# Hybrid four-mixer layer: v and z of mixer C as a seven-product unit, rope matmuls issued one by one, B's levels merged by predicated copies, output projection as seven products

## The chip, the cores and the metric

The kernel runs on 1 core of one Trainium2 chip. Its time is the device time of one execution in microseconds, the median of the runs shown. All data is float32, and every logical matmul is issued to the array as two instructions, so the profile counts two matmuls for one in the code.

## What is computed

Two layers (`DEPTH = 2`) on a sequence of 1024 rows of width 1024. Each layer does, cut to what matters here:

```python
h = _rmsnorm(x, norm_g[l])
p = h @ w_in[l]                       # all input projections and the merge gates
oa = _chunk_band_attention(...) * silu(az)
ob = _hgrn2(...) * silu(bz)           # mixer B, a decayed linear recurrence in chunks of 64
oc = _dsa(_rope(cq), _rope(ck), cv, _rope(cqi), _rope(cki), cwi) * silu(cz)   # indexer, top 256 keys, attention
od = _rwkv7(...) * silu(dz)
y = sum over branches of sigmoid(g) * (o @ w_branch[l, b])
x = x + y @ w_out[l]                  # output projection, 1024 x 1024 by 1024 x 1024
```

and after both layers a last RMSNorm.

## The kernel before

The normalised input stands transposed in `hT` (128 partitions, 8 blocks of the model width, 1024 rows), the weights pass through the ring `wr` of four slots of 256 columns. The engines' programs are written by hand, one list for each engine and layer, in the order C, D, B, A of the mixers, and then the tail. They meet at semaphores. `Jobs` keeps PSUM banks: `open` waits until the bank was emptied, `filled` signals the reader, `emptied` gives it back. Banks G[0] and G[1] (512 columns each) take the products of projections in turn, T and O and the pair S2 the mixers' small work.

**Fills.** Projections that no mixer waits for at once are cut into fill units of one 512-column matmul (or two 256-column ones), and `pe_fill(pe, n)` issues the next n of them wherever TensorE (PE) would else wait for another engine. Numbers in the constants (`TOPK_FILL`, `QK_FILL`, `D_FILL`, `B_FILL`) say how many at each place; `FILL_ORDER` says in which order projections come, and the merge gates take the rest. What is left after mixer A is issued in one run in `pe_tail`. Most fills are done by a scheme of seven products for a 2 by 2 block product (`PRODUCTS`), in place of eight: four matmuls to a product, with block sums of the weights (`t1` to `t4`) and of `hT` (`s1` to `s4`) made by GpSimd (POOL) in `pool_w_sums` and `pool_h_sums`. ScalarE (ACT) drains the products in `act_fills`, up to the mark at which it stands in its own program, and POOL adds half of them to their places. "Rows" units are two blocks of 256 columns (v and z of a mixer) as 256-column matmuls with four pairs of row tiles.

**Mixer C.** PE projects the index key, the index queries (blocks `("C", 0)`, `("C", 1)`, in `pe_proj_t`), then v and z (blocks 2 and 3, `pe_proj_n`, 64 matmuls of 512 columns). `pe_rope` makes the rotated half of a tile by one matmul into the single bank T, which VectorE (DVE) or, for q and k, ACT and POOL, must empty before the next. Then come the index scores: `for n, (i, hp, c, w) in enumerate(index_units)`, with 2 fills at each second unit. DVE sums them over heads, then searches the 256th largest score of each row bit by bit from 31 to 0 (six counts over up to 1024 columns and three small instructions for a bit), while PE issues fills; then PE starts the attention (`scores`, `turn`, `values`), whose first softmax on DVE needs the search done.

**Mixer B.** For each half m: decayed keys and queries for six levels (DVE differences, ACT exponentials, `L1499`), state sums (`adds`), a scan of 15 linked steps over chunks, then for each of 8 row tiles seven small product blocks, one for a level and one for the diagonal. DVE multiplies all seven by 0/1 masks (`near7`) and adds them up (L1591 and L1598); PE multiplies the result with v.

**Tail.** 64 branch products (two matmuls each) go through four banks; DVE multiplies each with its gate and adds it into `yT`, the half of the rows first. Then the output projection: for each of 8 row tiles two column halves by eight matmuls of 512 columns, DVE adds the old x (L914), and ACT and DVE make the next norm in `act_norm` and `dve_norm`.

## Time and profile before

| | |
|---|---|
| median of 3 runs | 3275.61 us (3271.96 to 3279.4) |
| profiled execution | 3285.09 us, its span 3283.1 us |
| PE busy | 3003.6 us, 91% of the span |
| DVE, ACT, POOL busy | 1661.7, 823.4, 658.9 us |
| mean granted TensorE clock | 0.968 |
| PE waits for ACT's drain of a probability tile (L971) | 51.1 us in 71 waits |
| PE waits for B's merged tile (L1463) | 21.1 us in 24 waits |
| PE waits before rope matmuls (L1217) | 31.1 us |

Busy time is a union over overlapping instructions, so a group's busy time divided by its count is the pitch at which it streamed; the mean duration beside it contains the latency of the array. PE is the engine with the least idle time, but it is not idle evenly: it stands at places where one of its small results goes through DVE or ACT and back.

### The profile page before, as it was taken

The page shows a single profiled execution, that of the slowest core. Times are in us where ns is not written, and L with a number is a line of the kernel's source. Part 1 is how long each engine was busy: PE and PEld are TensorE (multiplying, and loading weights), DVE is VectorE, ACT ScalarE, POOL GpSimd, SP SyncE. Part 2 cuts the span into 40 slices and gives each one's busy share as a digit, 9 for nine tenths or more (in the row PEclk, how much of TensorE's full clock was granted, in tenths as well). Part 3 has the DMA queues.
Part 4 walks back from the last instruction along what each step waited for, and adds up shares of the span by engine and source line. Part 5 has one row for each costly group of instructions (what it writes and reads, how often), then busy time and mean ns, then how long its engine had stood idle before and what let it go on. Part 6 is the DMA issues. An engine that isn't in the chain of part 4 may idle for free. (4 is left out here: it accounts for less than half of the span.)

```text
span 3283.1 us, 46212 instructions
## 1 busy us (share of the span) xinstructions
PE 3003.6 (91%) x18760; PEld 1547.7 (47%) x18760; DVE 1661.7 (51%) x3186; ACT 823.4 (25%) x1554; POOL 658.9 (20%) x476
## 2 busy tenths in 40 slices
PE   6999997999998889899989999879999887898997
PEld 3444444457543446444443444444665444554443
DVE  2169974753347741254112799748333577222632
ACT  2032134321124223400110411443211242244000
POOL 1014530231112223100010064203211221321000
PEclk9999999999999999999999999998999999999998
DMA  5001120110111131063040011101001111211721
GB/s 206 15 16 39 39 67 11 39 40 28 44 37 64 31 112 37 33 231 105 0 148 16 13 39 46 61 21 41 28 28 53 49 42 57 93 49 49 233 68 58
DMA packets 132346, 195.79 MB, mean 60 GB/s; under 512 B 8072, under 2 KB 87976, under 8 KB 131880
## 3 DMA queue, kind: packets, MB, share of 16 engines
q1 hardware_dynamic: 113544, 158.74, 14.9%
q10 hardware_dynamic: 18592, 34.09, 2.8%
q8 instruction: 152, 2.49, 0.3%
q14 instruction: 58, 0.48, 0.0%
HBM read 146.14 MB, written 48.78 MB: 59 GB/s over the span
## 5 line engine op out<-in xcount | busy, mean ns | idle before, releaser
L505 PE MATMUL ps<-hT,wr 128*128 128x512 f32 x1600 | 764.0, 617 | 12.7 <-ACT wr L551 11.2
L505 PEld LDWEIGHTS ps<-hT,wr 128*128 128x128 f32 x1600 | 299.3, 196 | 342.2 <-issue 315.7
L505 PE MATMUL ps<-sums,wr 128*128 128x512 f32 x800 | 386.6, 620 | 18.4 <-ACT arena L560 9.3
L1361 DVE TENSOR_SCALAR_CACHE_REDUCE arena<-arena,sm 128x384 f32<-128x384 f32 (+5 forms) x384 | 337.9, 942 | 2.2
L650 POOL TENSOR_TENSOR gts<-gts,wr 128x512 f32<-128x512 f32 x96 | 133.8, 1394 | 739.9 <-ACT wr L551 565.1
L505 PEld LDWEIGHTS ps<-sums,wr 128*128 128x128 f32 x800 | 152.4, 198 | 194.4 <-issue 168.9
L1049 DVE CUSTOM_DVE_ANT_0 arena<-ps,arena 128x640 f32<-128x640 f32 (+7 forms) x128 | 90.4, 706 | 271.3 <-PE ps L960 210.2
L740 PE MATMUL ps<-wr,hT 128*128 128x512 f32 x512 | 220.1, 592 | 0.0
L728 PE MATMUL ps<-xo,arena 128*128 128x512 f32 x512 | 220.1, 592 | 0.0
L505 PE MATMUL ps<-wr 128*128 128x512 f32 x400 | 190.2, 608 | 0.0
L551 ACT ACTIVATE wr<-ps 128x512 f32<-128x512 f32 x150 | 89.3, 595 | 376.3 <-PE ps L505 356.2
L625 POOL TENSOR_TENSOR wr<-wr 128x512 f32<-128x512 f32 (+1 forms) x54 | 77.7, 1438 | 454.7 <-PE ps L505 346.3
L728 PEld LDWEIGHTS ps<-xo,arena 128*128 128x128 f32 x512 | 97.3, 190 | 122.5 <-issue 122.5
L740 PEld LDWEIGHTS ps<-wr,hT 128*128 128x128 f32 x512 | 97.3, 190 | 122.5 <-issue 122.5
L971 PE MATMUL ps<-con,arena 128*128 128x128 f32 x528 | 97.5, 289 | 55.4 <-ACT arena L1034 51.1
L1024 ACT ACTIVATE arena<-arena,sm 128x640 f32<-128x640 f32 (+7 forms) x128 | 94.1, 735 | 149.1 <-DVE sm L1054 148.8
L838 ACT ACTIVATE arena<-arena 128x1024 f32<-128x1024 f32 x24 | 25.4, 1056 | 422.6 <-DVEq L916 418.7
L971 PEld LDWEIGHTS ps<-con,arena 128*128 128x128 f32 x528 | 59.4, 142 | 133.7 <-issue 82.6
L914 DVE SCALAR_TENSOR_TENSOR arena<-ps,arena 128x1024 f32<-128x1024 f32 x16 | 19.6, 1225 | 190.1 <-PE ps L740 190.1
L570 ACT ACTIVATE gts<-ps 128x512 f32<-128x512 f32 x96 | 57.1, 595 | 231.6 <-PE ps L505 221.5
L505 PEld LDWEIGHTS ps<-wr 128*128 128x128 f32 x400 | 74.4, 194 | 81.5 <-issue 79.8
L427 PE MATMUL ps<-hT,wr 128*128 128x512 f32 x256 | 112.0, 598 | 0.0
(294 smaller groups left out, 4449.6 us busy)
## 6 DMA issues: line engine op xcount, KB each, us to landing
wr<-in_w_in SPq DMA_DIRECT2D x68, 1024.0 KB, 5.3
gate_tanh<-gts ACTq DMA_DIRECT2D x128, 256.0 KB, 2.0
arena<-gate_tanh SPq DMA_DIRECT2D x128, 256.0 KB, 3.0
x_cur<-arena SPq DMA_DIRECT2D x2, 4096.0 KB, 23.5
arena<-in_w_branch SPq DMA_DIRECT2D x8, 1024.0 KB, 5.9
wr<-in_w_out SPq DMA_DIRECT2D x8, 1024.0 KB, 6.6
arena<-x_cur SPq DMA_DIRECT2D x4, 2048.0 KB, 8.3
arena<-in_x SPq DMA_DIRECT2D x4, 1024.0 KB, 8.1
```

What stands on the lines that cost most here:

```text
L427: ins = pe.matmul(ap, lhsT=wr[:, n % 2, kt, P * m:P * m + P], rhs=hT[:, kt, 512 * half:512 * half + 512], start=kt == 0, stop=kt == KT - 1)
L505: ins = pe.matmul(ap, lhsT=right(u, w_side)[:, kt, :], rhs=left(h_side, kt), start=fresh and kt == 0, stop=kt == half_k - 1, skip_group_ch ...
L551: jobs.emptied(act.activation(stage_of(u), src, ACT.Copy), key)
L570: jobs.emptied(act.activation(gts[:, slot, :], src, ACT.Copy), key)
L625: pool.tensor_tensor(t1, b12, right(u, "b11"), ALU.subtract).then_inc(sg("w_sums"), 1)
L650: pool.tensor_tensor(dst, dst, stage_of(u), ALU.add).then_inc(sg("pool_added"), 1)
L728: ins = pe.matmul(ap, lhsT=wbs[ORDER.index(b)][:, k2, P * ct:P * ct + P], rhs=xo[:, 2 * ORDER.index(b) + k2, 512 * half:512 * half + 512], ...
L740: ins = pe.matmul(ap[:, 512 * j:512 * j + 512].rearrange("p (a c) -> p a c", a=2), lhsT=yT[:, kt, P * i:P * i + P], rhs=wr[:, 2 * j:2 * j ...
L971: ins = pe.transpose(ap[:, P * j:P * j + P], rows[u % 2][:, P * (g + j):P * (g + j) + P], ident)
L1024: act.activation(r, r, ACT.Exp, bias=neg[:, u % 2:u % 2 + 1], accum_out=tot[:, u % 8:u % 8 + 1]).then_inc(sg("probs_" + b), 1)
L1049: ins = dve.tensor_tensor_reduce(out=rows[u % 2][:, 0:P * nb], in0=ap[:, 0:P * nb], in1=bias(i, h, nb), scale=HD ** -0.5, scalar=-3e38, op ...
L1361: ins = dve.tensor_scalar(compared[i], iscore[i], cbits[:, j:j + 1], None, ALU.is_ge, ALU.add, accum_out=count[:, j:j + 1])
```

## The change

1. v and z of mixer C leave the start of the layer and become a rows unit of seven products in `FILL_ORDER`, behind q and k of C. Their drain, adds and the silu of z (`z_tanh`, one tanh of 2048 columns on ACT, one instruction on DVE at bit 4 of the search) move along. `TOPK_FILL` goes from 144 to 92.
2. Rope matmuls are issued one by one, between the 8-matmul products of the query projection or with 3 fills (`ROPE_FILL`) behind each.
3. In B, the multiply of seven blocks and the reduction become one multiply and six predicated copies, each linked to the one before by a semaphore. ACT drains the fills behind `adds` one product at a time between its level exponentials.
4. In D, 12 fills are marked for ACT ahead of its square root (`norm`), and 16 instead of 24 follow.
5. The output projection becomes seven products of four 512-column matmuls for each of four pairs of row tiles. POOL makes the sums of `w_out` (16 instructions) and of `yT` (16 instructions) in `pool_tail`; the branch pieces are ordered so that column blocks k and k+4 finish together; DVE adds each product to x in seven instructions per pair of row tiles.

```diff
-TOPK_FILL = 144
+TOPK_FILL = 92
 QK_FILL = 8
+ROPE_FILL = 3
...
-... "P": 1, "S": 1, "turn": 24}
+... "P": 1, "S": 1, "norm": 12, "turn": 16}
...
-        tail = [(half, ct, b) for half in range(2) for ct in range(KT) for b in ORDER]
+        tail = [(half, ct, b) for half in range(2) for k in range(KT // 2) for ct in (k, k + KT // 2) for b in ORDER]
...
-            for i in range(NT):
-                if i == 0:
-                    pe.wait_ge(sg("out_w_loaded"), 16 * 4)
-                if i % 4 == 0:
-                    pe.wait_ge(sg("y_piece"), 32 * (i // 4 + 1))
-                key = ("out", i)
-                ap = jobs.open(pe, key, S2[i % 2])
-                for j in range(2):
-                    for kt in range(KT):
-                        ins = pe.matmul(...)
+            pe.wait_ge(sg("out_w_loaded"), 16 * 4)
+            pe.wait_ge(sg("y_piece"), len(tail))
+            for i in range(NT // 2):
+                for p, (y_side, w_side, fresh) in enumerate(PRODUCTS):
+                    key = ("out", i, p)
+                    ap = jobs.open(pe, key, G[p % 2])
+                    if w_side in FIRST_T and not i:
+                        pe.wait_ge(sg("out_w_sums"), half_k * FIRST_T[w_side])
+                    if y_side[0] == "s" and not i:
+                        pe.wait_ge(sg("y_sums"), 4 * half_k if y_side == "s4" else 3 * half_k)
+                    for kt in range(half_k):
+                        ins = pe.matmul(ap..., lhsT=out_left(y_side, kt)[:, P * i:P * i + P], rhs=out_right(w_side, kt), ...)
+                    jobs.filled(ins, key)
...
+        def pool_tail(pool):
+            pool.wait_ge(sg("out_w_loaded"), 16 * 4)
+            ...
+            for kt in range(half_k):
+                pool.wait_ge(sg("y_piece"), last_of[1, kt + half_k] + 1)
+                pool.tensor_tensor(L("s3", kt), L("a11", kt), L("a21", kt), ALU.subtract).then_inc(sg("y_sums"), 1)
+                ...
...
-                pe_proj_t(pe, "C", 1)
-                pe_rope(pe, "qi0")
-                pe_proj_n(pe, "C", 2, 2)
-                pe_rope(pe, "qi1")
+                pe_proj_t(pe, "C", 1, [lambda pe, m=m, half=half: pe_rope(pe, "qi0", m, half) for m in range(2) for half in range(2)])
+                for m in range(2):
+                    for half in range(2):
+                        pe_rope(pe, "qi1", m, half)
+                        pe_fill(pe, ROPE_FILL)
...
+                pe_fill_until(pe, "fills z", ("C", 2))
                 pe_fill(pe, TOPK_FILL)
...
+                    if bit == 4:
+                        dve.wait_ge(sg("z_tanh_C"), 1)
+                        dve.scalar_tensor_tensor(H(6, 2), z_tanh, 1.0, H(6, 2), ALU.add, ALU.mult)
...
-                    pe_fill(pe, B_FILL["adds"])
-                    jobs.mark(("B adds", m))
+                    for n in range(B_FILL["adds"] // 4):
+                        pe_fill(pe, 4)
+                        jobs.mark(("B adds", m, n))
...
                         if n >= 2:
-                            act_fills(act, ("khn", m))
-                    act_fills(act, ("B adds", m))
+                            act_fills(act, ("B adds", m, n - 2))
...
-                        ins = dve.tensor_tensor(masked, ap.rearrange(...)[:, :, 0:LEVELS + 1], each, ALU.mult)
...
-                        dve.tensor_reduce(att_t[i % 2], masked.rearrange("p e n t -> p e t n"), AX, ALU.add).then_inc(sg("att_ready"), 1)
+                        link(dve, dve.tensor_tensor(att_t[i % 2], product[:, :, 0], near[:, 0]..., ALU.mult))
+                        for n in range(1, LEVELS + 1):
+                            ins = dve.copy_predicated(att_t[i % 2], near[:, n].bitcast(I32)..., product[:, :, n])
+                            if n < LEVELS:
+                                link(dve, ins)
...
+                pe_fill(pe, D_FILL["norm"])
+                jobs.mark("norm D")
                 pe_fill(pe, D_FILL["turn"])
...
+                act_fills(act, "norm D")
                 act.wait_ge(sg("d_var"), 1)
```

What this moves on PE, from the projection of the index key to the index scores. Before (L427 is the query projection, L1217 rope, L443 v and z, L478 fills, L1250 index scores):

```order
L427 MATMUL ps<-hT,wr 128x512 x32
L1234 MATMUL ps<-con,arena 128x8 x8
L1217 MATMUL ps<-arena,con 64x512 x2
L427 MATMUL ps<-hT,wr 128x512 x32
L1217 MATMUL ps<-arena,con 128x512 x4
L443 MATMUL ps<-wr,hT 128x512 x64
L1217 MATMUL ps<-arena,con 128x512 x4
L478 MATMUL ps<-hT,wr 128x512 x2
L1250 MATMUL ps<-arena 128x384 x4
```

The same stretch of the changed kernel, from the last product of the query projection on (L1252 is rope, L462 fills, L1289 index scores):

```order
L427 MATMUL ps<-hT,wr 128x512 x8
L1252 MATMUL ps<-arena,con 128x512 x2
L462 MATMUL ps<-hT,wr 128x512 x3
L1252 MATMUL ps<-arena,con 128x512
L462 MATMUL ps<-hT,wr 128x512 x3
L1252 MATMUL ps<-arena,con 128x512
L462 MATMUL ps<-hT,wr 128x512 x3
L1252 MATMUL ps<-arena,con 128x512
L462 MATMUL ps<-hT,wr 128x512 x5
L1289 MATMUL ps<-arena 128x384 x4
```

The 64 matmuls of v and z are gone from here, and 12 fills stand between the last four ropes. Up to C's attention the program before issues 256 fill units, the changed one 252, of which 56 are v and z; in the whole layer there are 860 before and 916 now.

On DVE, in B, one row tile before (L1591 multiplies, L1598 reduces), and the end of the scan ahead of it:

```order
L1582 SCALAR_TENSOR_TENSOR arena<-arena,sm,ps 128x64 x15
L1584 ISA
L1585 ISA
L1591 TENSOR_TENSOR arena<-ps,con 128x896
L1598 TENSOR_REDUCE arena<-arena 128x128
L1591 TENSOR_TENSOR arena<-ps,con 128x896
L1598 TENSOR_REDUCE arena<-arena 128x128
```

and two row tiles now:

```order
L1640 TENSOR_TENSOR arena<-ps,con 128x128
L1642 COPY_PREDICATED arena<-con,ps 128x128 x6
L1647 ISA
L1640 TENSOR_TENSOR arena<-ps,con 128x128
L1642 COPY_PREDICATED arena<-con,ps 128x128 x6
L1647 ISA
```

Two instructions over 896 elements became seven over 128.

On PE at the end of the layer, the output projection of the changed kernel (before it was one row, `L740 MATMUL ps<-wr,hT 128x512 x128`), for the first of four pairs:

```order
L713 MATMUL ps<-xo,arena 128x512 x128
L727 MATMUL ps<-wr,hT 128x512 x8
L727 MATMUL ps<-sums 128x512 x4
L727 MATMUL ps<-arena,hT 128x512 x4
L727 MATMUL ps<-wr,arena 128x512 x8
L727 MATMUL ps<-gts,hT 128x512 x4
```

A pair takes 28 matmuls in place of 32; the third product is the first that reads sums.

## Rows read from the trace of the kernel before

**Rows 1.** The page: busy time by engine, and the granted clock in 40 slices.

```profile
PE 3003.6 (91%) x18760; PEld 1547.7 (47%) x18760; DVE 1661.7 (51%) x3186; ACT 823.4 (25%) x1554; POOL 658.9 (20%) x476
...
PEclk9999999999999999999999999998999999999998
```

**Rows 2.** Groups by line and shape: busy us, mean ns, idle before, releaser.

```profile
L740 PE MATMUL ps<-wr,hT 128*128 128x512 f32 x512 | 220.1, 592 | 0.0
L443 PE MATMUL ps<-wr,hT 128*128 128x512 f32 x256 | 110.2, 592 | 0.0
...
L1598 DVE TENSOR_REDUCE arena<-arena 128x128 f32<-128x896 f32 x32 | 54.0, 1686 | 1.1
L1591 DVE TENSOR_TENSOR arena<-ps,con 128x896 f32<-128x896 f32 x32 | 34.9, 1092 | 38.5 <-PE ps L1450 35.9
L1997 DVE TENSOR_TENSOR arena<-ps,arena 128x128 f32<-128x128 f32 x32 | 9.3, 292 | 44.5 <-PE ps L1807 44.5
```

**Rows 3.** Timeline of PE, last index ropes, layer 0: start, us, instructions [idle before].

```profile
178.63 2.08 PE L1217 MATMUL ps<-arena,con 128*128 128x512 f32 x2 [3.66 <-DVE arena L1320]
181.49 2.08 PE L1217 MATMUL ps<-arena,con 128*128 128x512 f32 x2 [0.78 <-DVE arena L1320]
185.68 3.78 PE L478 MATMUL ps<-hT,wr 128*128 128x512 f32 x4 [2.11 <-DVE arena L1323]
```

**Rows 4.** Timeline of PE, last rope of q, layer 0.

```profile
303.43 2.07 PE L1217 MATMUL ps<-arena,con 128*128 128x512 f32 x2 [2.10 <-ACT arena L1291]
```

**Rows 5.** Timeline of PE, a rows unit issued without a break (A's v and z), layer 0.

```profile
1227.74 3.69 PE L502 MATMUL ps<-wr,hT 128*128 128x256 f32 x16 [2.18 <-DMA wr<-in_w_in]
1232.68 1.97 PE L502 MATMUL ps<-wr,sums 128*128 128x256 f32 x8 [1.25 <-POOL wr L627]
...
1241.95 3.62 PE L502 MATMUL ps<-wr,hT 128*128 128x256 f32 x16
...
1254.03 3.62 PE L502 MATMUL ps<-wr,hT 128*128 128x256 f32 x16
```

**Rows 6.** Timeline of DVE, first index sum and end of the search, layer 0.

```profile
191.48 0.42 DVE L1346 TENSOR_SCALAR arena<-arena,sm 128x384 f32<-128x384 f32 x1 [5.86 <-ACT arena L1283]
...
454.48 0.16 DVE L1366 COPY sm<-ps 128x6 int32<-128x6 int32 x1
```

**Rows 7.** Timeline of PE, query projection's start and attention's first transpose, both layers.

```profile
50.05 27.63 PE L427 MATMUL ps<-hT,wr 128*128 128x512 f32 x64
...
464.99 0.27 PE L971 MATMUL ps<-con,arena 128*128 128x128 f32 x1
...
1676.70 27.63 PE L427 MATMUL ps<-hT,wr 128*128 128x512 f32 x64
...
2089.23 0.27 PE L971 MATMUL ps<-con,arena 128*128 128x128 f32 x1
```

**Rows 8.** Timelines of DVE and PE in B, layer 0.

```profile
1073.34 4.71 DVE L1582 SCALAR_TENSOR_TENSOR arena<-arena,sm,ps 128x64 f32<-128x64 f32 x15
...
1070.24 5.40 PE L505 MATMUL ps<-sums,wr 128*128 128x512 f32 x8 [4.64 <-ACT arena L560]
...
1094.07 0.38 PE L1463 MATMUL ps<-xo,arena 64*64 64x64 f32 x5 [0.59 <-DVE arena L1598]
...
1108.59 0.69 PE L1463 MATMUL ps<-xo,arena 64*64 64x64 f32 x8 [2.44 <-DVE arena L1598]
```

**Rows 9.** Timeline of DVE, last instruction of D's norm, layer 0.

```profile
994.09 3.25 DVE L2020 TENSOR_TENSOR arena<-arena 128x2048 f32<-128x2048 f32 x1
```

**Rows 10.** Branch products, layer 0: window's busy time by engine; DVE's last add.

```profile
1470.00:1529.00 59.00, 59.00 (x139) 26.17 (x138) 41.29 (x61) 0.00 (x0) 0.00 (x0) 1.00 0.48 147
...
1530.31 0.69 DVE L758 TENSOR_TENSOR hT<-hT,arena 128x512 f32<-128x512 f32 x1
```

**Rows 11.** Timelines of POOL and DVE at the last index ropes, layer 0.

```profile
172.19 4.51 POOL L612 TENSOR_TENSOR wr<-hT,sums 128x2048 f32<-128x2048 f32 x1 [122.32 <-PE ps L443]
...
173.71 3.54 DVE L1322 TENSOR_TENSOR arena<-arena,xo 128x512 f32<-128x512 f32 x1
```

More of the change, by code:

```diff
@@ L261, in gated_merge_kernel @@
         ring, at = [], {}
-        for b, js in (("C", range(4)),):
+        for b, js in (("C", range(2)),):
             for j in js:
@@ L429, in pe_proj_t @@
                     jobs.filled(ins, key)
+                    behind[2 * m + half](pe)
             block_done[n] = key
-        def pe_proj_n(pe, b, j, nb):
-            n = at[b, j]
-            for k in range(nb):
-                w_wait(pe, n + k)
-            assert n % 2 + nb <= 2
-            for i in range(NT):
-                key = (b, j, i)
-                ap = jobs.open(pe, key, gbank(pe))
-                for kt in range(KT):
-                    o = ap[:, 0:NCB * nb].rearrange("p (a c) -> p a c", a=nb)
-                    ins = pe.matmul(o, lhsT=hT[:, kt, P * i:P * i + P], rhs=wr[:, n % 2:n % 2 + nb, kt, :],
-                                    start=kt == 0, stop=kt == KT - 1)
-                jobs.filled(ins, key)
-            for k in range(nb):
-                block_done[n + k] = key
         fill_at = [0, 0]
@@ L904, in act_o_turn, with add, rows_step @@
             jobs.emptied(ins, ("oT", b, i))
+        pair_rows = [i + 4 * n for i in range(NT // 2) for n in range(2)]
         def dve_out(dve):
-            dve.wait_ge(sg("xr_loaded"), 16)
-            def rows_step(i):
-                if i == 4:
-                    dve.wait_ge(sg("xr2_loaded"), 16)
-                ap = jobs.ready(dve, ("out", i))
-                xr = xin[:, i, :]
-                ins = dve.scalar_tensor_tensor(xr, ap, 0.5, xr, ALU.mult, ALU.add)
-                jobs.emptied(ins, ("out", i))
+            def add(i, p, t, n, first=None):
+                key = ("out", i, p)
+                ap = jobs.ready(dve, key)
+                if first is not None:
+                    jobs.stored(dve, ("out", i, first))
+                xr = xin[:, t, 512 * n:512 * n + 512]
+                jobs.emptied(dve.scalar_tensor_tensor(xr, ap, 0.5, xr, ALU.mult, ALU.add), key)
+            dve.wait_ge(sg("xr_loaded"), 16)
+            def rows_step(r):
+                i = r // 2
+                if r % 2:
+                    add(i, 6, i + 4, 0)
+                    jobs.stored(dve, ("out", i, 6))
+                else:
+                    add(i, 0, i, 0)
+                    add(i, 1, i, 0, 0)
+                    add(i, 2, i, 1)
+                    if i == 0:
+                        dve.wait_ge(sg("xr2_loaded"), 16)
+                    add(i, 3, i + 4, 1)
+                    add(i, 4, i + 4, 1, 3)
+                    add(i, 5, i, 1, 2)
+                    jobs.stored(dve, ("out", i, 5))
                 dve.engine_nop().then_inc(sg("new_rows"), 1)
-            dve_norm(dve, "next", rows_step)
+            dve_norm(dve, "next", rows_step, pair_rows)
         ssq, msq, root, inv = small(8), small(8), small(8), small(8)
@@ L1291, in act @@
                     jobs.emptied(act.activation(qk_turned[n % 2], ap, ACT.Copy), key)
+                act_fills(act, "fills z")
+                unit_done(act, ("C", 2))
+                act.wait_ge(sg("qk_roped"), len(qk_rope))
+                act.activation(z_tanh, H(6, 2), ACT.Tanh, scale=0.5).then_inc(sg("z_tanh_C"), 1)
                 att[1](act)
@@ L2043, in _ @@
             def _(act):
-                act_norm(act, "first", sg("rows_in"))
+                act_norm(act, "first", sg("rows_in"), range(NT))
             @block.vector
```

160 lines of the change are left out of this document (90 added, 70 removed).

## The prediction, made before the result was known

> **What bounds the kernel.** I read the page first: PE is busy 91% and no other engine above 51% [rows 1], so the time is PE's stream plus the places where PE waits or runs slow. The groups by shape give the stream's price: a 512-column matmul costs 220.1/512 = 0.43 us an instruction, so 0.86 us in the code [rows 2]. The timeline of PE shows the waits: where a result goes from bank T through DVE and back, PE idles 3.66, 0.78 and 2.11 us, and the instructions between last 2.08 us for two, where two at full rate take 0.86 and their latency [rows 3]. The granted clock there was at the lower of its two levels (1.2 GHz, half). Last I followed DVE in C, since PE's fills only cover its search: sums begin at 191.48 and the search ends at 454.6 [rows 6], PE's attention begins its first transpose at 464.99 [rows 7]. So before, DVE was ready some 8 us ahead of PE. A fill unit is work that must be done somewhere; a change gains only if it takes work out of PE's stream or puts work where PE idled.
>
> **Output projection.** 256 instructions a layer become 4 x 28 x 2 = 224: -13.8 us. PE used to go straight from the branch products to the projection, because its first four tiles need only the first half of y. Now it waits for all 64 pieces. DVE's last add ran 1530.31 to 1531.0 [rows 10]; it follows PE's last branch matmul by a multiply and an add of 0.69 us and their hand-overs, so +1.8 us. The sums behind it are covered: POOL's 2048-column sum takes 4.51 us [rows 11], a quarter about 1.2 us (estimate), three for the last blocks 3.6 us, and PE has two products (6.9 us) before the first sum. s4 is due after five products, 17 us. The last add shrinks from 1024 to 512 columns, -0.5 us. Sum -12.5 a layer, -25.0 in all.
>
> **v and z, and the ropes of C.** v and z cost 128 instructions or 55.1 us a layer [rows 2]. As a rows unit they are 224 instructions of 256 columns. In A's unit 56 of these took 1254.03 - 1241.95 = 12.08 us, 0.216 each [rows 5]: 48.3 us. This saves 6.8 us, the full eighth, since a half-wide matmul streams at half the price. Against that stands the switch into a rows unit issued without a break: 2.18 us for its weights and 1.25 us for the 1024-column sums [rows 5], +0.3 for a drain; +3.7.
>
> But PE is not what ends this stage. I follow both engines from the query projection's start, 50.05 [rows 7]. PE: 128 instructions of projection 55.0, six ropes inside 5.2, transposes 0.6, four ropes with 3 fills each 4 x 3.44 = 13.8. The index scores start at 124.6 instead of 185.7. DVE: its first sum came 5.8 us after PE's start of that phase; 1.9 of it was the half clock (3.78 us for four instructions, rows 3), so now 128.5. From there to the search's end it needs what it took, 454.6 - 191.5 = 263.1, +2.3 for the silu of z (2048 columns), +1.5 for POOL's in-place sum of hT, which now falls into the index sums. That gives 395.5, and about 2 us later PE's first transpose: 397.5. PE's own arrival: from 185.7 to 465.0 it took 279.3. Take off 16 fill units (13.7), the idle at q's and k's ropes (2 x 3.5: the 2.10 of [rows 4] and two of 0.69 ahead of it), and what isolated and half-clock instructions lost there (5.8, of it 1.9 in rows 3's last), and add the switch (3.7): 256.5, so PE is there at 381. **PE will stand some 16.5 us in front of C's attention, waiting for the search**: 92 is too few fills here. Covering the whole with 20 more would have been free.
>
> The stage so ends 67.5 us earlier in layer 0, and 65.1 in layer 1 (412.5 us from rows 7 where layer 0 has 414.9). In exchange 252 units are done where 256 were, of which 56 are v and z: 60 units of other work are left for later, 51.5 us. Net -16.0 and -13.6. After such a wait I expect the lower clock at the attention's start: +2 each, an estimate from the two instructions at 2.08 us in place of 1.0 behind a 3.66 us wait [rows 3]. Sum -25.6. This takes in all that the ropes lost (their idle and the half clock): most of it becomes the new wait.
>
> **D.** DVE's norm chain ends at 997.3 [rows 9], and PE's turn starts right then, its 24 fills and a wait behind it. Four more fills go in (-3.4), but ACT now drains the third product before its square root, and loads its table behind it; I take 2.3 us on DVE's chain. Net -1.1 a layer, -2.2.
>
> **B.** *Adds.* PE idled 4.64 us from 1065.6 because ACT did not drain [rows 8]. With the marks ACT drains between levels, but then each exponential waits for a product (3.43 us). The third product is full at 1065.6 + 2 x 3.43 = 1072.5, drained at 1073.1; only then comes the sixth exponential (1.1), DVE's last pair of products (1.2), the query's (1.2) and the scan (4.7): 1081.3, where it ended at 1078.05 [rows 8]. PE waits for it there. It passed before with 13 more units behind 1070.24, 11.2 + 1.8 for the half clock, at 1083.2: -1.9. I take -1.5 in the second half, -3.4 a layer. *Merge.* A row tile took DVE 1.09 + 1.69 + gaps = 2.91 us [rows 2], of which PE waited 0.59 [rows 8], so its own work is 2.3. No row shows a predicated copy of 128 elements from PSUM. Its bounds: a multiply of 128 elements takes 0.292 us; if it streams like the reduction (1686/896 = 1.88 ns an element), 0.40 us [rows 2]. I take 0.292 as the nearest shape, with 0.03 a link: 7 x 0.325 + 0.15 = 2.4. Then 0.5 goes from each of some 12 waits a layer, the last of 2.44 us among them: -5.9. With 0.40 the step is 3.1 us and PE loses 0.2 on 16 steps: +3. B in all -18.6. The Trainium skill (VectorE: DVE Perf Modes, the trn2 errata) gives a PSUM-source DVE instruction 120 cycles and one per element at 0.96 GHz; by that the copy would be 0.26 us, the step PE-bound, and the sum 3 us lower. No run here shows it yet.
>
> **Sum.** -25.0 - 25.6 - 2.2 - 18.6 = -71.4 on 3285.1, so 3213.7. The median stood 9.5 us below the profiled run, 0.997 of it: **3204 us**.
>
> **A rule that speaks against it.** DVE's product of two SBUF operands took 3.54 us at 173.71 while POOL's 4.51 us sum ran; the add of the same 512 columns in the tail, with POOL idle, took 0.69 [rows 10, 11]. The tail puts 32 POOL sums beside DVE's adds. The Trainium skill (SBUF — State Buffer, Who interferes with whom) says that a DVE instruction with two SBUF inputs and a GpSimd one that reads SBUF exclude each other for the whole instruction; the trace agrees. In rows: DVE is busy 41.29 of 59 us in the branch phase [rows 10], 33 us of slack in 110. POOL's 28 sums before the last piece are 33 us at 1.2. Blocked for all of it, DVE would be just level with PE, at +1 to +4 us a layer: rival 4.
>
> **Rivals.**
> 1. *The copies are dear* (0.40 us). For: a third operand, the mask. Against: the multiply, too, reads two. B's merge gives +3 instead of -5.9 a layer: 3222. If they cost 0.5, 3240.
> 2. *No wait at C.* DVE's sums or search end earlier, or PE is held up elsewhere by fills it would do anyway; half or all of the 16.5 us and the clock are kept: 3185 to 3167. Against: DVE's own chain from the first sum takes 263 us and none of it is shortened.
> 3. *Slower than before: the index sums don't start earlier.* Place: start of index scores. If doubled keys, fill weights or bank T hold it at 186 as before, C ends where it did with 60 units undone and 2.3 more on DVE: +54 a layer instead of -15, in all about 3340. It decides at a delay of some 36 us of the 61. For: nothing but the number of things that must arrive; the key copy is issued once two ropes are done, 30 us ahead.
> 4. *Tail loses to the port* or another small new wait (POOL behind on q's and k's ropes, ACT held at `qk_roped` with both G banks full), 5 to 15 us a layer: 3215 to 3235.
>
> **Chances.** Forecast (3192 to 3213) 0.55; rival 1 0.13; rival 2 0.10; rival 3 0.02; rival 4 0.20. The range 3172 to 3237 leaves out rival 3, the dear end of 1 and the far end of 2. A measurement here tells 0.2% (6.5 us) from no change. Every case but rival 3 is below 3269: faster 0.95, same 0.02, slower 0.03.
>
> **What would show it.** 224 instructions of L727 at 0.43 us and a gap of about 2 us ahead; ropes with no idle above 1 us; a PE wait of 13 to 20 us for the first probability tile in each layer, with DVE busy all through; B's step near 2.4 us with copies of 0.29; ACT's sixth exponential later by 4 us; D's square root 2 us later. Wrong if the wait at C is missing or above 30, if copies exceed 0.35, or if POOL's or DVE's instructions in the tail stretch so that PE waits in the branch products.

## The result, and the profile after

The changed kernel took **3238.12 us** (median of 4 runs, 3237.72 to 3244.4) where the kernel before took 3275.43 (4 runs): ratio 0.989, 95% interval 0.9873 to 0.9907. It is 37 us faster. I had forecast 71 us (3204, in a range of 3172 to 3237); the direction held, the size was half, and the time lies 1 us above my range.

The page of the changed kernel, busy time by engine and granted clock in 40 slices; its span is 3242.2 us:

```profile
PE 2942.4 (91%) x18888; PEld 1573.8 (49%) x18888; DVE 1699.3 (52%) x3372; ACT 836.9 (26%) x1580; POOL 811.0 (25%) x572
...
PEclk9999999999988899999999999999999898999998
```

Beside [rows 1] PE is busy 61 us less and the span is 41 us less: PE now idles 20 us more. POOL is busy 152 us more. The chain of waits of PE (total us, times, longest):

```profile
PE ps L1483 <- DVEq L1629: 28.7, 4, 7.9
PE ps L1007 <- ACT arena L1060: 23.9, 4, 10.7
...
PE ps L1711 <- DVE arena L1941: 17.7, 2, 8.8
...
PE ps L862 <- DVEq L2073: 12.4, 2, 6.2
...
PE ps L727 <- DVE arena L933: 4.7, 6, 0.8
```

I had expected the second of the five. The others are not in the list of the kernel before: L1483 is B's first matmul on the states, L1711 D's head sums, L862 D's turn, L727 the output projection. To see where the forecast and the trace part, I follow PE by landmarks. Each number is after minus before in us, counted from the layer's first projection matmul:

| landmark on PE | forecast, layer 0 / 1 | layer 0 | layer 1 |
|---|---|---|---|
| C's first transpose | -67.5 / -65.1 | -64.7 | -62.3 |
| D's first value transpose | -65.5 / -63.1 | -60.2 | -56.8 |
| D's turn | -63.2 / -60.8 | -57.7 | -54.4 |
| B's last turn | -72.5 / -70.1 | -60.6 | -59.2 |
| first branch product | -24.4 / -22.0 | -11.3 | -11.3 |
| end of the output projection | -36.9 / -34.5 | -20.0 | -19.9 |

A layer misses by 17 and 15 us: 3 at C's search, 3 in C's attention and D's start, 6 and 5 in B, 1 and 0 behind it, 4 in the output. Each landmark is one profiled execution against one: kernels that are the same up to D still differ by 2 to 4 us there, because the granted clock doesn't fall at the same places. The table says where to look, and the runs below decide.

PE at C, its wait for the search (timeline: start, us, instructions [idle before]):

```profile
388.61 1.98 PE L489 MATMUL ps<-sums,wr 128*128 128x512 f32 x4
399.94 0.48 PE L1007 MATMUL ps<-con,arena 128*128 128x128 f32 x1 [9.36 <-ACT arena L1060]
```

The transpose stands at 399.94 (forecast 397.5), but PE had come at 390.6 (forecast 381): the wait is 9.4 us in place of 16.5, and 10.7 in layer 1. Two waits for ACT that my sum did not have make up 5.5 of the 9.6 us by which PE was late: 3.4 us inside the unit of v and z, where I had 0.3, and 2.4 at the index scores. The search ended 2.8 us late, counted from the layer's start: DVE's first sum came 1.6 later than forecast, and from there to the end it took 268.9 us, not 266.9.

### The profile page after: what moved, and what is told of

The parts are those of the page before. It is cut to its first block and busy times, and to the rows that moved or that the text cites. A ratio compares the mean times of both kernels' runs of the same rounds, so it can differ in the third digit from the quotient of the medians.

```text
span 3242.2 us, 46848 instructions
## 1 busy us (share of the span) xinstructions
PE 2942.4 (91%) x18888; PEld 1573.8 (49%) x18888; DVE 1699.3 (52%) x3372; ACT 836.9 (26%) x1580; POOL 811.0 (25%) x572
## 5 line engine op out<-in xcount | busy, mean ns | idle before, releaser
L489 PE MATMUL ps<-hT,wr 128*128 128x512 f32 x1600 | 758.3, 612 | 3.7 <-ACT wr L535 3.7
L489 PE MATMUL ps<-sums,wr 128*128 128x512 f32 x800 | 374.1, 602 | 0.0
L635 POOL TENSOR_TENSOR gts<-gts,wr 128x512 f32<-128x512 f32 x96 | 144.7, 1507 | 705.2 <-ACT wr L535 575.9
L486 PE MATMUL ps<-wr,hT 128*128 128x256 f32 x576 | 144.9, 397 | 8.8 <-DMA wr<-in_w_in 8.8
L1007 PEld LDWEIGHTS ps<-con,arena 128*128 128x128 f32 x528 | 60.2, 144 | 154.9 <-issue 83.3
L486 PEld LDWEIGHTS ps<-wr,hT 128*128 128x128 f32 x576 | 109.8, 196 | 31.3 <-issue 13.6
L933 DVE SCALAR_TENSOR_TENSOR arena<-ps,arena 128x512 f32<-128x512 f32 x56 | 38.8, 692 | 151.1 <-PE ps L727 151.1
L1390 DVE SCALAR_TENSOR_TENSOR arena<-arena,sm 128x512 f32<-128x512 f32 (+3 forms) x140 | 105.8, 756 | 21.6 <-ACT arena L1322 17.3
```

Source lines behind the costliest of these rows:

```text
L486: ins = pe.matmul(ap[:, 0:NCB], lhsT=left(h_side, kt)[:, P * i:P * i + P], rhs=right(u, w_side)[:, kt, :], start=fresh and kt == 0, stop=k ...
L489: ins = pe.matmul(ap, lhsT=right(u, w_side)[:, kt, :], rhs=left(h_side, kt), start=fresh and kt == 0, stop=kt == half_k - 1, skip_group_ch ...
L635: pool.tensor_tensor(dst, dst, stage_of(u), ALU.add).then_inc(sg("pool_added"), 1)
L1007: ins = pe.transpose(ap[:, P * j:P * j + P], rows[u % 2][:, P * (g + j):P * (g + j) + P], ident)
L1390: ins = dve.scalar_tensor_tensor(acc, r, wgt, acc, ALU.mult, ALU.add)
```

## Experiments

All times below are medians; each ratio compares a run with the kernel before on the same chip. The runs were made on several chips, on which the kernel before took 3275.4 to 3279.1 us, so two medians of different chips can lie up to 3.7 us apart for that alone. Where it matters, the difference with this taken off stands beside it.

### Four single edits

**fill_104:**

```diff
-TOPK_FILL = 92
+TOPK_FILL = 104
```

> The changed kernel with 12 more fill units ahead of C's attention (TOPK_FILL 104). Forecast's theory (too few fills, PE stands idle for the search): the waits of 9.36 and 10.7 us at L1007 go, the 12 units (10.3 us a layer) are no longer to do later: span 3242.2 - 20 = 3222, and up to 4 less if the lower clock behind the wait goes too. Rival (what ends C's attention is DVE or ACT, so that a later start is made good or lost elsewhere): 3235 to 3242.

3199.2 us, ratio 0.9762 (0.9743 to 0.978): 39 us faster than the changed kernel, where the theory of the forecast gave 20 to 24 and its rival at most 7. C's first transpose came 0.8 us later and the wait was gone, as forecast. But D's head sums came 8.6 us earlier in layer 0 and 3.7 in layer 1, and the wait at L1711 had vanished with no more fills there. That was the surprise to explain.

**b_marks_undone:**

```diff
-                    for n in range(B_FILL["adds"] // 4):
-                        pe_fill(pe, 4)
-                        jobs.mark(("B adds", m, n))
+                    pe_fill(pe, B_FILL["adds"])
+                    jobs.mark(("B adds", m))
...
-                            act_fills(act, ("B adds", m, n - 2))
+                            act_fills(act, ("khn", m))
+                    act_fills(act, ("B adds", m))
```

> The changed kernel with one mark behind all 16 fills of B's adds, ACT as before. Theory from the two traces (the marks hold the exponentials back, so that the scan ends 8 us behind PE): from B's first key transposes to its first state matmuls PE lost 4 us in the first half and 2 in the second against before; undone the waits of 7.88 and 7.04 us at L1483 go, the 4.64 us wait for ACT returns: 12 us faster, span 3230. Rival, the forecast's own term (marks gain 3.4 us a layer): 7 us slower, 3249.

3233.95 us, 0.9867 (0.9849 to 0.9886). From B's first key transposes to the branch products PE gained 6.4 us in layer 0 and 3.5 in layer 1; the span fell by 6.6, since C's attention happened to be 3 us longer in layer 1. The waits at L1483 are gone. The medians alone differ by 4 us, less than their uncertainty; the trace carries this one. In the changed kernel ACT and DVE stood like this (timelines, layer 0):

```profile
1018.44 1.05 ACT L1544 ACTIVATE arena<-arena 128x1024 f32<-128x1024 f32 x1
...
1019.52 1.59 DVE L1615 TENSOR_TENSOR arena<-arena 128x512 f32<-128x512 f32 x1 [2.12 <-ACT arena L1544]
...
1025.10 4.71 DVE L1626 SCALAR_TENSOR_TENSOR arena<-arena,sm,ps 128x64 f32<-128x64 f32 x15
...
1030.03 1.98 PE L1483 MATMUL ps<-arena 64*64 64x64 f32 x64 [7.88 <-DVEq L1629]
```

The last exponential runs at 1018.44 behind a drain, DVE's scan at 1025.10, and PE waits 7.88 us for it. POOL summed beside DVE's last products (its timeline, same kernel):

```profile
1019.30 1.26 POOL L612 TENSOR_TENSOR wr<-wr 128x512 f32<-128x512 f32 x1
1020.52 1.71 POOL L613 TENSOR_TENSOR wr<-wr 128x512 f32<-128x512 f32 x1
1022.20 1.71 POOL L635 TENSOR_TENSOR arena<-arena,wr 128x512 f32<-128x512 f32 x1
```

With the marks undone (the layer so far within 0.2 us) the scan began at 1016.99:

```profile
1016.99 4.71 DVE L1626 SCALAR_TENSOR_TENSOR arena<-arena,sm,ps 128x64 f32<-128x64 f32 x15
```

and PE went into the state matmuls at 1026.93 without a wait.

**merge_undone** puts back one multiply of 896 elements and one reduction.

```diff
-                        link(dve, dve.tensor_tensor(att_t[i % 2], product[:, :, 0], ...))
-                        for n in range(1, LEVELS + 1):
-                            ins = dve.copy_predicated(att_t[i % 2], near[:, n]..., product[:, :, n])
+                        ins = dve.tensor_tensor(masked, ap..., each, ALU.mult)
+                        dve.tensor_reduce(att_t[i % 2], masked.rearrange("p e n t -> p e t n"), AX, ALU.add)
```

> The changed kernel with B's levels merged by one multiply and one reduction as before. Forecast's term: 5.9 us a layer, span 3254. What the two traces suggest (the state-to-turn stretch shrank by 5.7 and 4.3 us in the halves): 10 us a layer, span 3262. If the copies had gained nothing: 3242.

3252.85 us, 0.9928 (0.9908 to 0.9947): the merge is worth 14.7 us by the medians; by the traces, from D's end to the branch products, 3.9 and 6.8, so 10.7. My 11.8 lies between the two. The copies, by line and shape in the changed kernel:

```profile
L1642 DVE COPY_PREDICATED arena<-con,ps 128x128 f32<-128x128 int32 x192 | 58.1, 302 | 6.6
L1640 DVE TENSOR_TENSOR arena<-ps,con 128x128 f32<-128x128 f32 x32 | 9.3, 292 | 19.8 <-PE ps L1495 16.0 <-DVEq L1647 0.2
```

0.302 us a copy: the nearest shape, 0.292, had been the right bound to take, and rival 1 (0.40) is out. The 0.26 us that the prediction set beside it is too low, for the copy and for the multiply of this shape (0.292).

**out_undone** puts back the single product, the old order of the branch pieces and no sums.

```diff
-                for p, (y_side, w_side, fresh) in enumerate(PRODUCTS):
+                for j in range(2):
+                    for kt in range(KT):
```

> The changed kernel with the output projection as one product of 256 instructions a layer. Forecast's term: 12.5 us a layer, span 3267. What the two traces suggest (from the branch products' start to the layer's end the shift went from -11.3 to -20.0): 8.7 us a layer, span 3259.6; the missing 3.8 being DVE's drain at each pair's turn (0.78 x 3), the wait ahead and a longer start. If the tail's sums also slow the branch products, their 110 us fall too.

3256.02 us, 0.9943 (0.9922 to 0.9963): the seven products are worth 17.9 us, 8.8 and 8.7 a layer by the traces (109.9 us from the branch products' end against 101.2). I had forecast 12.5 a layer; 0.5 of that was for DVE's last add and falls behind the last of these landmarks.

### The bank behind the output projection's wait

**bank_swap:**

```diff
-                    ap = jobs.open(pe, key, G[p % 2])
+                    ap = jobs.open(pe, key, G[(i + p) % 2])
```

> The changed kernel with the output projection's banks taken in turn over the pairs too, so that the first product of a pair does not open the bank that the last product of the pair before just filled. Theory: the six waits of 0.78 us at L727 for DVE go, span 4.7 us less, 3237.5. Rival (DVE's drains are late anyway, the wait moves to the second product): 3242.

The changed kernel's output projection (timeline of PE), where product 6 of a pair and product 0 of the next share a bank:

```profile
1519.40 7.11 PE L727 MATMUL ps<-wr,hT 128*128 128x512 f32 x16 [1.65 <-issue]
...
1540.08 3.60 PE L727 MATMUL ps<-gts,hT 128*128 128x512 f32 x8
1544.46 7.13 PE L727 MATMUL ps<-wr,hT 128*128 128x512 f32 x16 [0.78 <-DVE arena L933]
```

and the same place in bank_swap:

```profile
1536.68 3.60 PE L727 MATMUL ps<-gts,hT 128*128 128x512 f32 x8
1540.11 7.03 PE L727 MATMUL ps<-wr,hT 128*128 128x512 f32 x16
```

From 1540.08 to 1544.46 are 4.38 us, in bank_swap 3.43: a turn cost 0.95, three a layer. The phase shrank by 3.1 us in each layer, 6.2 in all (I expected 4.7); the median is 3234.91, 0.9868 (0.9851 to 0.9884), which is 3.2 us below the changed kernel's, 6.9 with the chips' difference taken off.

### What the C part is worth alone

**c_alone** keeps v, z and the ropes of the change and puts back output projection, merge, B's marks and D's fills; **c_alone_104** has TOPK_FILL 104 besides.

```diff
-D_FILL = {... "norm": 12, "turn": 16}
+D_FILL = {... "turn": 24}
...
-                act_fills(act, "norm D")
```

> Of the change only v, z and the ropes in C; the output projection, D's fills, B's marks and B's merge are as before. Forecast's term: -25.6 us on 3285.1, a time of 3259.5. What the two traces suggest (D's end stands 60 and 57 us ahead, 51.5 us of units are due later, some of it lost by new waits): -14 us, 3271.

> c_alone with TOPK_FILL 104. c_alone was 3 us faster than before in the medians, 12 in the spans. Units and wait alone: 20 us less than c_alone, 3256 median. If the C part brings its forecast 25 us once the wait and what follows it are gone, and no other part of the change is needed for it: 3276 - 39 as from the changed kernel to fill_104, 3237.

c_alone: 3276.05 us, ratio 0.9994 (0.9984 to 1.0004), no change that the measurement tells, where I had forecast 25.6. By the traces it gained 7.0 and 3.9 us in the layers (-14.0 and -11.6 by my own landmarks up to there, the 60 units taken off); the profiled execution of before stood 9.5 above its median, so the medians are the better judge. c_alone_104: 3250.82 us, 0.9913 (0.9892 to 0.9934). Twelve fills more are worth 25 us even without the rest of the change.

**d_undone** puts back only D's fills (the edit above, in the changed kernel).

> The changed kernel with D's turn as before: 24 fills, no mark behind 12 of them, ACT not draining ahead of its square root. Forecast's term: 2.2 us slower in all. What c_alone's trace suggests (D's turn 32.1 us behind the last state with 24 units, 30.4 with 28 in the changed kernel; PE waits 4.6 and 2.6 us for ACT there and is at the lower clock behind it): 10 us slower, span 3252, median 3248.

3238.73 us, 0.9877 (0.9858 to 0.9896): D's part brings nothing that the medians tell. My second number was wrong: D's turn did come 1.6 us later behind the last state (32.1 us with 24 fills, 30.5 with 28), with PE waiting 4.6 us for ACT again, but it was given back before the branch products (shift -7.2 there in layer 0, against -3.4 at D): from D's turn to B's it took 178.2 and 178.6 us in place of 185.4 and 183.6. So without the mark D's turn is as long here as in c_alone; but c_alone_104 has no mark either, and its D's turn takes 28.7. What is lost there depends on which fills come to stand in it.

### Why twelve fills gave 39 us

**warm_24** and **warm_12** cover the wait with work that nobody needs:

```diff
                 pe_fill(pe, TOPK_FILL)
+                ap = jobs.open(pe, "warm", T)
+                for n in range(12):
+                    ins = pe.matmul(ap, lhsT=con[:, 0:P], rhs=con[:, 512:1024], start=True, stop=True)
+                jobs.filled(ins, "warm")
```

> The changed kernel with 24 matmuls of 512 columns (10.3 us) that nobody needs, behind the fills and ahead of the wait for C's search: they cover the wait as the 12 more units of fill_104 did, but no fill is taken from later. fill_104 gave 43 us of span (39 in the medians) where its units and the wait explain 20. Theory of the clock (the wait ahead of C's attention costs more in the half clock behind it than the 2 us a layer forecast): this run gains too, 5 to 8 us a layer in C's attention, span 3226 to 3232. Theory of the fill stream's place (12 more fills ahead move POOL's sums off DVE's first work of D, where the wait of 8.83 us at L1711 stood): this run keeps that wait and the span stays at 3236 to 3242.

> As warm_24, but with 12 matmuls of 512 columns: each shows as two instructions of 0.43 us, so 24 of them took 20.6 us, not 10.3, and the wait was overshot. 12 take 10.3 us and just cover the wait. From warm_24, where C's attention gained 4.8 and 2.8 us on its own and the wait of 8.8 us at D's head sums stayed as it was, the theory of two separate losses expects: first transpose within 1.5 us of the changed kernel's, C's attention 5 and 3 us shorter, the D wait still 8.8 us in each layer, span 3234. If the wait in D came from the half clock behind C's wait, it goes too: 3216.

warm_24: 3256.52 us, 0.9936 (0.9913 to 0.9959). Its expectation had the price of a matmul wrong by two, so that it moved C's attention back by 11.1 and 9.6 us; the attention then took back 4.8 and 2.8. warm_12: 3233.5 us, 0.9866 (0.9843 to 0.9889), a median 4.6 us lower (7.5 with the chips' difference taken off), a span 11.4 lower. C's first transpose stood as in the changed kernel (+0.8, -0.1), C's attention was 4.9 and 3.3 us shorter, the wait of 8.8 us at D's head sums stayed. The attention's reason shows in windows over it (start and end, length, busy of PE, PEld, DVE, ACT, POOL with counts, PEclk, DMA share, GB/s), the changed kernel first:

```profile
400.00:529.00 129.00, 105.12 (x616) 57.72 (x616) 67.58 (x164) 62.84 (x137) 12.58 (x9) 0.92 0.05 17
```

then fill_104:

```profile
400.00:524.00 124.00, 98.75 (x618) 54.00 (x617) 68.10 (x166) 62.98 (x139) 12.71 (x10) 0.99 0.08 27
```

The same matmuls (616 and 618 records) make PE busy 105.1 us at a granted clock of 0.92 and 98.8 at 0.99. From within the 9.4 us in which PE stood, the clock was at the lower level (1.2 GHz) for some 14 us, and again for 7 and twice 3 in the attention; with the wait covered, either way, most of that was gone in layer 0.

One execution against one misleads here. Eight of the kernels run (the changed one, the four single undoings b_marks, merge, out and d, bank_swap, c_alone and kk_20) are the same up to D's start. From the first transpose to DVE's first shift of D they took 121.1 to 125.3 us in their two layers, 122.8 in the mean, with 9.4 to 21.1 us at the lower clock. The seven whose first transpose comes with the wait covered and no units added behind it (warm_12, warm_24, fill_104, c_alone_104, pool_load, combined_1, combined_2) took 119.0 to 122.2, 120.1 in the mean, with 3.4 to 13.7 us at the lower clock. So the clock behind this wait costs 2.7 us a layer; I had priced it at 2, which was nearly right.

That leaves D's start. The same kind of window, from DVE's first shift of D to its product ahead of the head sums, the changed kernel:

```profile
524.70:554.80 30.10, 20.63 (x46) 7.75 (x44) 29.50 (x27) 12.08 (x17) 12.25 (x6) 0.92 0.14 44
```

and fill_104:

```profile
519.70:546.10 26.40, 25.26 (x46) 9.60 (x44) 25.81 (x27) 11.45 (x17) 2.94 (x2) 0.81 0.08 30
```

The same 27 instructions keep DVE busy 29.5 us in the one and 25.8 in the other. POOL is busy 12.3 us in the one, 2.9 in the other (12.3 in c_alone, whose stretch was 30.1 us; 4.7 before, where it was 27.4). Layer 1 shows the same: DVE's chain took 30.0 us in both layers of the changed kernel and 26.3 in both of fill_104. POOL and DVE of the changed kernel side by side:

```profile
529.28 2.24 POOL L613 TENSOR_TENSOR wr<-wr 128x512 f32<-128x512 f32 x1
531.49 2.24 POOL L635 TENSOR_TENSOR gts<-gts,wr 128x512 f32<-128x512 f32 x1
...
530.50 2.11 DVE L1926 SCALAR_TENSOR_TENSOR xo<-arena,par,xo 128x1024 f32<-128x1024 f32 x1
532.64 2.17 DVE L1924 TENSOR_TENSOR arena<-xo 128x1023 f32<-128x1023 f32 x1
...
537.55 1.28 DVE L1926 SCALAR_TENSOR_TENSOR xo<-arena,par,xo 128x1024 f32<-128x1024 f32 x1
538.87 1.22 DVE L1924 TENSOR_TENSOR arena<-xo 128x1023 f32<-128x1023 f32 x1
```

While POOL sums, DVE's shifts take 2.11 and 2.17 us, otherwise 1.28 and 1.22, and POOL's sums take 2.24 where one alone takes 1.27. The Trainium skill (SBUF — State Buffer, Who interferes with whom) says that a VectorE instruction with two SBUF inputs and a GpSimd instruction that reads SBUF exclude each other. The trace agrees: the two engines' instructions end in turn, POOL at 531.52, DVE at 532.61, POOL at 533.73, DVE at 534.81, some 1.1 us apart, as they would if each began its work only when the other's was done. A sum costs DVE 0.9 us and not the whole 1.27, since part of it has passed when DVE's instruction comes.

That is still not the whole 39 us. I counted fill_104 against the mean of the changed kernel, bank_swap and out_undone, which are the same up to the branch products but for the output projection. Its first branch product came 20.6 us earlier a layer. D's head sums came 5.1 earlier. To D's turn it took 3.0 less: 1.6 right behind the head sums, where the changed kernel is at the lower clock for 5.6 us behind its wait and fill_104 is not, and 1.7 in D's turn. To B's turn it took 3.9 less (6.0 and 1.8 in its two layers); and behind that 8.5 less, where the 12 units, 10.3 us, are missing. The gain in B was not taken apart.

**fill_98** and **fill_112** (TOPK_FILL 98 and 112) move the fill stream by other amounts.

> TOPK_FILL 98: 6 units more ahead of C's attention. The wait falls from 9.4 to 4.2 us. Theory of cover alone: 10.3 us less in all, half of the clock's 5 and 3 us: median 3238 - 14 = 3224. Theory of the place: of the sums on POOL beside DVE's first work of D, the three weight sums fall 6 units earlier, into C's attention, the fourth stays: DVE's chain there 27 to 28 us in place of 30.0, the wait at the head sums 6 us or less, 4 to 6 us more off in all: 3219.

> TOPK_FILL 112: 8 units more than fill_104, all behind the end of the search, so that C's attention starts 4.6 to 7 us later and the 16 units are done there in place of later. Theory of cover alone: as fill_104, 3199, within 3. Theory of the place: the next unit's three weight sums fall on DVE's first work of D, its chain is 28 to 30 us again (26.3 in fill_104), a wait of some us stands at the head sums: 3203 to 3209.

fill_112: 3201.64 us, 0.9765 (0.9749 to 0.9782). Its wait at L1711 is back:

```profile
PE ps L1711 <- DVE arena L1941: 17.0, 2, 8.5
```

since the three weight sums of the next unit now fall on DVE's shifts (542.3 to 548.9; DVE's chain runs from 526.7 to 555.8, 29.1 us). The time is still only 2.4 us above fill_104's, inside the cover theory's 3 us and just under the range of the place theory, so this run does not tell them apart: the units done at C's late start and this wait nearly balance. fill_98: 3236.69 us, 0.9874 (0.9857 to 0.989), **nothing gained** where both theories gave 14 or more. Its waits at C fell to 5.1, PE's way from its first work of D to the head sums was shorter by 2.1 (DVE's chain 27.3 in place of 30.0, as the place theory had it), but C's attention grew by 5.5 us in layer 0 and 11.4 in layer 1, at the same granted clock of 0.92, with longer waits for ACT's drains there (L1050: 22.1 us in 28 waits in place of 16.6). That is outside all that the eight equal kernels show. Why that place of the stream is so bad for the attention was not tested.

**pool_load** puts POOL work beside DVE in D and leaves the fills alone:

```diff
-TOPK_FILL = 92
+TOPK_FILL = 104
...
+                pool_fills(pool, ("fills", "D"))
+                pool.wait_ge(sg("wd_shifted"), 1)
+                for n in range(14):
+                    link(pool, pool.tensor_tensor(H(22.25, 0.25), con[:, 0:256], con[:, 256:512], ALU.add))
                 pool_fills(pool)
```

> fill_104 with 14 sums of 256 columns on POOL that nobody needs, from the moment DVE has made its first shift of D. Theory of POOL beside DVE: DVE's chain to the head sums takes 29 to 31 us in place of 26.3, its products of two SBUF operands show 2.1 to 2.3 us in place of 1.2 to 1.3 while they run, PE waits 3 us or more at the head sums in each layer: median 3199 + 6 to 8 = 3206. Rival (the place of the fills itself): chain 26.3, median 3199 within 3.

3209.39 us, 0.9785 (0.9772 to 0.9798), 10 us above fill_104, 8 with the chips' difference taken off. The window is 30.4 us long again:

```profile
519.50:549.90 30.40, 20.52 (x47) 7.77 (x45) 29.84 (x26) 11.90 (x17) 26.61 (x16) 0.93 0.07 26
```

and in the chain of waits

```profile
PE ps L1715 <- DVE arena L1945: 19.0, 2, 9.5
```

PE waits at the head sums. POOL's 14 sums and two of DVE's instructions beside them:

```profile
522.20 23.82 POOL L1354 TENSOR_TENSOR arena<-con 128x256 f32<-128x256 f32 x14 [13.39 <-DVE arena L1930]
...
523.35 1.57 DVE L1930 SCALAR_TENSOR_TENSOR xo<-arena,par,xo 128x1024 f32<-128x1024 f32 x1
524.95 1.63 DVE L1928 TENSOR_TENSOR arena<-xo 128x1023 f32<-128x1023 f32 x1
```

DVE's chain took 30.3 us in both layers, where fill_104 has 26.3. So POOL's work beside DVE, with the fills left where they are, is enough to lengthen D's start by what the changed kernel lost there (3.7) and to bring the wait back. It is more POOL work than the changed kernel has there (26.6 us against 12.3), so the size is not a copy of it; for that the rows of the changed kernel speak.

**kk_20** (20 fills in place of 10 ahead of the head sums) asks whether such a wait may simply be filled.

> The changed kernel with 20 fill units in place of 10 ahead of D's head sums, where PE waits 8.83 us for DVE in each layer. Theory (any wait of PE may be filled with units at no cost): 8.8 us a layer, and 1 to 2 us of the half clock behind it: span 3242.2 - 20 = 3222. Rival (the place of the fill stream decides more than the wait, since POOL's sums fall on other work of DVE): off that by 5 us or more to either side.

3221.18 us, 0.9828 (0.9806 to 0.9849): 17 us, 20 with the chips' difference taken off, what the waits and the clock behind them cost, as the first theory said.

### The best version

**combined_1:** TOPK_FILL 104, B's marks undone, the banks in turn, D's turn 24. **combined_2** has 20 and 16 in place of 12 and 24; **combined_3** is combined_1 with TOPK_FILL 112.

```diff
-TOPK_FILL = 92
+TOPK_FILL = 104
...
-"norm": 12, "turn": 16}
+"norm": 12, "turn": 24}
```

> The changed kernel with TOPK_FILL 104, B's marks undone, the output banks in turn and D's turn fills 24 in place of 16. fill_104's span 3198.8, less 7 for the marks, 4.7 for the banks, and the two waits of 4.6 us at L862 (the 8 units are done there in place of later): 3178. If the gain of fill_104 came from a chance place of the fills, some of it is lost again: 3185 to 3200.

> combined_1 with D's fills 20 ahead of the mark and 16 behind in place of 12 and 24: ACT drains the 20 before it waits for the variance, so that PE's waits for ACT at L489 (14.4 us in all, up to 5.7) go. The units are the same. Span 3182 - 11 = 3171; if ACT's square root then comes late instead (it must drain two more products first, 3.4 us each of PE time): 3182.

> combined_1 with TOPK_FILL 112. By the theory of the place it is worse than combined_1 by the same as fill_112 is against fill_104: 3182 to 3188 median. By cover alone 3178 within 3.

combined_1: **3178.39 us**, 0.9691 (0.9675 to 0.9707), the fastest here, 101 us below before on its chip; its 36 fills behind the last state of D fill the 31 us that DVE's norm needs. combined_2: 3189.9 us, 0.9734 (0.9712 to 0.9755), slower, by the mechanism of its second case but with a span of 3186.8 where that case had 3182: ACT's square root ran 18.5 us behind PE's last state matmul where it ran 12.1 behind it in combined_1, and PE waited 6.0 us in each layer for the norm. combined_3: 3196.24 us, 0.9747 (0.973 to 0.9763), 18 us worse than combined_1; the place theory had the sign and 4 to 10 of it, and the rest is not explained. Its waits at L1711 are 8.5 us, and a wait for weights of 5.5 us has come that combined_1 does not have.

## Why the prediction was right and wrong

**The sum by its terms** (both layers; measured by undoing the part in the changed kernel, for C by doing it alone):

| part | forecast | medians | by the trace |
|---|---|---|---|
| output projection | -25.0 | -17.9 | -17.5 |
| C: v, z, ropes | -25.6 | -3.1 | -10.9 |
| D | -2.2 | -0.6 | |
| B, adds | -6.8 | +4.2 | +9.9 |
| B, merge | -11.8 | -14.7 | -10.7 |
| sum | -71.4 | -32.1 | |

The whole change gave -37.3. The terms add up to within 5 us of it, and each carries some 5 of uncertainty.

- **C's start and search: right in mechanism.** Ropes cost no idle, the index sums start 61 us earlier, and what ends the stage is DVE's search with PE waiting ahead of it. Covering the whole with more fills was free, as the text said. The wait was 9.4 and 10.7 us, not 16.5, because PE came 9.6 us later than the 381 forecast; the first transpose came 2.8 later.
- **C's term: the step that failed is "Net -16.0 and -13.6 ... +2 each".** It treated the 60 deferred units as a price alone, 0.86 us each, and left every later stage as long as it was. By the landmarks of c_alone it missed 7.0 and 7.6 us a layer. 2.7 of this is the later end of the search. C's attention and D's start together took what I had given them in layer 0 and 2.4 more in layer 1: POOL's sums made D's start 2.7 longer than before, 3.7 longer than in fill_104. The largest part, 4.2 and 4.0, lies between D's last state matmul and D's turn, a stretch that the forecast's C term left alone: 32.2 and 32.1 us in c_alone, against 28.0 and 28.1 before and 28.7 in c_alone_104, with the same 24 fills in all three. PE waits 7.2 and 7.5 us for ACT's drains there, in c_alone_104 and before 4.6, so the fills that now stand there are drained later; no run moved them alone. The rest, 0.3 and -0.4, is spread behind it. The clock behind C's own wait, 2.7 against 2, is not what failed. These 15 us stand against 22 by the medians. The two profiled executions differ by 10.3 us in their spans, where the medians differ by 3.1: the one of before stood 9.5 us above its median, and I took every duration from it. What of the missing 8 is a real loss stays open, and why the search ended later too.
- **D: right to put nothing much on it.** The sign and size can't be told from 0.
- **B's adds: the step "-1.9 ... -1.5" had the wrong sign.** Counted from the first matmul of `adds`, the sixth exponential was to run at +11.5 us and ran at +11.7: right. The scan was to end at +19.6 and ended at +23.1, because DVE's two last products took 1.59 and 1.75 us beside POOL's sums in place of 0.69, and the query's 2.28 in place of 1.2. The query's product had taken 2.29 us in the kernel before too, beside a POOL sum, so 1.1 of this was there to be read. PE was to arrive at +21.5 and arrived at +15.5: I had taken its arrival from before's, which had the 4.64 us stop for ACT in it, though the marks remove just that stop. -1.9 + 3.5 + 6.0 is 7.6, with a hand-over of 0.2 about the 7.9 us that PE waited; some 10 us at the lower clock followed. The 9.9 us in the table compare one execution with one. From D's turn to B's, five kernels with the same program there (the changed one, bank_swap, out_undone, warm_12, warm_24) take 182.9 to 185.5 us, 183.9 in the mean; b_marks_undone takes 181.2 and 180.7.
- **B's merge: right**, from the nearest row, and with the reason given: the copies took 0.302 us.
- **Output projection: -13.8 + 1.8 - 0.5 was mis-sized by 3.3 to 3.8 a layer.** The term that failed is the -13.8, which took every matmul at full stream: the phase went from 110.0 to 99.5 us, 10.5. 2.9 of the missing 3.3 is the bank of each pair's turn, which I never looked at (bank_swap gives 3.1 back). The gap ahead of the first product was 1.65, as forecast; POOL's tail sums cost the branch products nothing (110 us in both), so the port part of rival 4 did not happen where I put it. The two engines did get in each other's way in D and in B, where I did not look.
- **Rivals.** 1, 2 and 3 are out. 4 (small new waits, 3215 to 3235) is nearest to the result, and it should have had more than 0.20: the change adds or moves work on POOL, ACT and DVE at five places, and each new wait has one sign only.

## What to carry to other kernels

When fill work moves out of a stage, follow the fill stream onward through every later stage: each place where another engine has fixed work of its own (DVE beside POOL, ACT between two exponentials) meets other fills than before, and a stretch of 3.7 us there turned into a wait of 8.8. A wait of PE is best priced as its length plus the lower clock behind it (2.7 us behind C's wait of 9 to 11, 1.6 behind D's of 8.8), and filled up with work that must be done anyway (39 and 17 us for 12 and 10 fills here). It is not safe to count on it for any number: six fills more gave nothing (fill_98), so each place has to be run. Where an accumulation's banks alternate over an odd number of products, look at the turn.

## What the runs showed of the hardware

- A predicated copy of 128 fp32 elements from PSUM takes 0.302 us, 0.010 more than the multiply of the same shape.
- A POOL sum that runs with DVE's two-operand work costs both: 2.24 in place of 1.27 us on POOL, 2.17 in place of 1.22 on DVE. The 14 sums of 256 columns took 1.70 us each beside DVE's shifts, which went from 1.25 to 1.6. The instructions of the two engines end in turn, and many short sums stretch DVE less per instruction than long ones, but all along.
- In fill_104 PE's clock was lower in D's start (0.81 against 0.92), so that PE came later to the head sums and no wait showed, in 3.7 us less. A wait that vanishes from the list is not yet time gained; the landmark behind it tells.
